# The experts' down product in three one-pass products of high and low parts, in place of one plain product

## The reference

```python
def expert_block(args):
    xb, e = args          # 128 token rows, 1024 wide; weights 1024x512, 1024x512, 512x1024
    return (jax.nn.silu(xb @ w_gate[e]) * (xb @ w_up[e])) @ w_down[e]
```

## Time and profile before

| | |
|---|---|
| runs, us | 1544.82, 1678.39, 1680.1 |
| median of the runs | 1678.39 us |
| profiled execution, span from first to last instruction | 1678.9 us |
| TensorE busy | 1494.5 us (89%) |
| VectorE busy | 923.6 us (55%) |
| ScalarE busy | 586.6 us (35%) |
| DMA | 353.18 MB, mean 210 GB/s |
| mean granted TensorE clock | 0.857 |

### The profile page before, as it was taken

How to read it: one execution, slowest core, us unless ns; L and a number is a source line. 1 busy time by engine, 2 the same in 40 slices (tenths; PEclk the granted TensorE clock), 3 DMA queues, 4 the chain that set the end, 5 groups by cost and what they waited for, 6 DMA issues and landing times.

```text
span 1678.9 us, 15037 instructions
## 1 busy us (share of the span) xinstructions
PE 1494.5 (89%) x5233; PEld 977.5 (58%) x5233; DVE 923.6 (55%) x1344; ACT 586.6 (35%) x790; POOL 91.4 (5%) x133
## 2 busy tenths in 40 slices
PE   2899999399999998499989999999956999999892
PEld 2445455266667764288866666666535677766540
DVE  6588824667777771566642222222356777777304
ACT  1265002355555550322122222221234555555201
POOL 4000000100000000200000000000001000000001
PEclk9999999599999999699995555555977999999996
DMA  8946680369999987456370000000033999999644
GB/s 279 365 161 211 200 314 38 124 236 363 374 360 368 385 317 287 163 176 238 103 284 27 0 1 0 0 1 1 25 138 126 365 371 370 369 364 347 238 163 163
DMA packets 79747, 353.18 MB, mean 210 GB/s; under 512 B 12824, under 2 KB 13008, under 8 KB 70736
## 3 DMA queue, kind: packets, MB, share of 16 engines
q1 hardware_dynamic: 64704, 326.65, 52.6%
q0 software_dynamic: 8352, 20.46, 3.4%
q10 hardware_dynamic: 6640, 5.42, 1.0%
HBM read 334.15 MB, written 28.31 MB: 216 GB/s over the span
## 4 chain that ended last, share of the span: by engine, by line
PE 87%; DVE 6%; ACT 2%; DMA 2%; issue 2%; ACTq 1%; POOL 0%; DVEq 0%; POOLq 0%; SPq 0%
PE ps L1533 21%; PE ps L1544 14%; PE ps L1446 9%; PE ps L1632 8%; PE ps L1662 7%; PE ps L1474 7%; PE ps L1673 6%; PE ps L1687 4%; PE ps L1524 3%; PE ps L1519 2%; PE ps L1420 2%; PE ps L1538 1%; PE ps L1487 1%; PE ps L1456 1%; ACTq L636 1%
## 5 line engine op out<-in xcount | busy, mean ns | idle before, releaser
L1544 PE MATMUL ps<-slab_ring,scratch 128*128 128x512 f32 x560 | 246.5, 593 | 3.4 <-ACT scratch L783 2.1
L1533 PE MATMUL ps<-slab_ring_r,gate_rows_r 128*128 128x512 f32 x512 | 202.2, 395 | 0.0
L1544 PEld LDWEIGHTS ps<-slab_ring,scratch 128*128 128x128 f32 x560 | 105.8, 190 | 124.2 <-issue 117.3
L1229 DVE TENSOR_TENSOR slab_ring_r<-slab_ring,h_t_r 128x2048 fp32r<-128x2048 f32 x64 | 143.8, 2288 | 22.7 <-ACT h_t_r L735 22.7
L1364 DVE CUSTOM_DVE_ANT_0 mod_ring<-ps,log_count 128x512 f32<-128x512 f32 x64 | 44.2, 691 | 197.0 <-PE ps L1662 197.0
L1446 PE MATMUL ps<-h_t,slab_ring 128*128 128x512 f32 x320 | 146.1, 617 | 0.0
L1662 PE MATMUL ps<-h_t,scratch 64*128 64x512 f32 x128 | 127.4, 1106 | 0.9 <-DVE h_t L1355 0.9
L1632 PE MATMUL ps<-slab_ring_r 128*128 128x512 f32 x384 | 123.6, 404 | 1.7 <-DVE h_t_r L902 1.7
L817 ACT ACTIVATE mod_ring<-mod_ring,neg_max 128x512 f32<-128x512 f32 x64 | 46.2, 722 | 217.9 <-DVE neg_max L1365 217.9
L1533 PE MATMUL ps<-h_t_r,gate_rows_r 128*128 128x512 f32 x256 | 106.3, 415 | 14.7 <-DVE scratch_r L1223 14.7
L735 ACT ACTIVATE h_t_r<-slab_ring 128x2048 fp32r<-128x2048 f32 x64 | 118.4, 1901 | 0.2 <-issue 0.2
(11 more groups left out here) (286 smaller groups left out, 2200.2 us busy)
## 6 DMA issues: line engine op xcount, KB each, us to landing
slab_ring<-in_expert_w_gate_dram SPq DMA_DIRECT2D x35, 2048.0 KB, 10.3
slab_ring<-in_expert_w_up_dram SPq DMA_DIRECT2D x35, 2048.0 KB, 10.2
slab_ring<-in_expert_w_down_dram SPq DMA_DIRECT2D x35, 2048.0 KB, 10.4
mod_ring<-in_mod_w_dram SPq DMA_DIRECT2D x64, 512.0 KB, 4.7
y_rows<-scratch SPq DMA_DIRECT2D x35, 512.0 KB, 10.8
slab_ring<-in_mod_w_dram SPq DMA_DIRECT2D x32, 512.0 KB, 4.7
slab_ring<-in_w_qkv_dram SPq DMA_DIRECT2D x6, 2048.0 KB, 11.9
slab_ring<-in_w_in_ab_dram SPq DMA_DIRECT2D x5, 2048.0 KB, 19.3
```

Of the source, the lines that this page charges most:

```text
L1229: tt_(rest, w, top.bitcast(F32), ALU.subtract).then_inc(low_ready[c], 1)
L1533: ins = pe.matmul(ps[:, bank, :], x, w, start=(kt == 0 and i == 0), stop=(kt == KT - 1 and i == 2))
L1544: ins = pe.matmul(ps[:, 5 + h, :], hidT[:, f, :], w[:, 2 * f + h, :], start=(f == 0), stop=(f == FT - 1))
```

## The change

Down is split as gate and up are. Its slab gets a high part from ScalarE (in the buffer of the two, `XN_r` or `modr_r`, that up does not use in that layer) and a low part in place from VectorE, in two chunks each; both stand last in the queue of step e. The copy of the turned hidden out of PSUM now writes a high part (`hidT_high`), and VectorE computes a low part from PSUM minus this (`low_hid`), between the two chunks of low of up. TensorE does three one-pass products in place of each plain one, and waits for `hidt_low` and for the two low chunks of down in place of the slab. The overflow blocks keep the plain product. Some semaphores of the overflow code (`over`, `seen`) are merged into `turn_seen`.

```diff
--- before.py
+++ after.py
@@ -140,7 +140,9 @@
     ybuf = [R[:, 9:11, :].rearrange("p a n -> p (a n)"), R[:, 11:13, :].rearrange("p a n -> p (a n)")]
     xs_low = [R_r[:, i:i + 2, :].rearrange("p a (b n) -> p (a b) n", n=P) for i in (4, 13)]
     xs_high = [[G_r[:, g, :].rearrange("p (a n) -> p a n", n=P) for g in gs] for gs in ((0, 2), (1, 2))]
-    w_high = [[HT_r, (XN_r[:, :, :].rearrange("p t (h n) -> p (t h) n", h=2), modr_r)[l]] for l in range(LAYERS)]
+    XN_halves = XN_r[:, :, :].rearrange("p t (h n) -> p (t h) n", h=2)
+    w_high = [[HT_r, (XN_halves, modr_r)[l], (modr_r, XN_halves)[l]] for l in range(LAYERS)]
+    hidT_high, hidT_low = (R_r[:, i, :].rearrange("p (f n) -> p f n", n=P) for i in (8, 15))
     rt = R[:, 13:16, :].rearrange("p a n -> p (a n)")
     place_hot = R_r[:, 9:11, :].rearrange("p a (t n) -> p (a t) n", n=P)
     block_tok = R_r[:, 11, 0:2 * TT * WIDE].rearrange("p (a b) -> p a b", b=WIDE)
@@ -245,7 +247,8 @@
     xn_stored, place_ready, slots_summed, slots_ready = sem("xn_stored"), sem("place_ready"), sem("slots_summed"), sem("slots_ready")
     xs_filled = [sem("xs_filled0"), sem("xs_filled1")]
     xs_turned, xst_act, xst_dve = sem("xs_turned"), sem("xst_act"), sem("xst_dve")
-    high_ready, low_ready = [sem("gate_high"), sem("up_high")], [sem("gate_low"), sem("up_low")]
+    high_ready, low_ready = [sem("gate_high"), sem("up_high"), sem("down_high")], [sem("gate_low"), sem("up_low"), sem("down_low")]
+    hidt_low = sem("hidt_low")
     xs_high_ready, xst_turned, xst_split = sem("xs_high_ready"), sem("xst_turned"), sem("xst_split")
     gate_done, up_done, silu_done = sem("gate_done"), sem("up_done"), sem("silu_done")
     hid_ready, hid_turned, hidt_ready = sem("hid_ready"), sem("hid_turned"), sem("hidt_ready")
@@ -254,7 +257,7 @@
     turn_seen = sem("turn_seen")
     y_zeroed = sem("y_zeroed")
     comb_filled = [sem(f"comb_filled{t}") for t in range(TT)]
-    over = [{n: sem(f"over{l}_{n}") for n in ("wg", "wu", "wd", "xs", "turned", "xst", "gu", "silu", "hid", "hidt_in", "hidt", "down", "yb", "stored", "step", "over", "seen", "gate")}
+    over = [{n: sem(f"over{l}_{n}") for n in ("wg", "wu", "wd", "xs", "turned", "xst", "gu", "silu", "hid", "hidt_in", "hidt", "down", "yb", "stored", "step", "gate")}
             for l in range(LAYERS)]
     qkv_high, qkv_low, qkv_chunk = sem("qkv_high"), sem("qkv_low"), sem("qkv_chunk")
     ht_full, ht_high_act, ht_high_dve = sem("ht_full"), sem("ht_high_act"), sem("ht_high_dve")
@@ -459,7 +462,7 @@
                     sp.wait_ge(o["yb"], k + 1)
                     sp.dma_start(y_dram[bass.ds((k + NE) * P, P), :], ybuf[0]).then_inc(o["stored"], 16)
                     sp.wait_ge(o["stored"], (k + 2) * 16)
-                    sp.sem_inc(o["over"], 1)
+                    sp.sem_inc(turn_seen, 1)
             for par in range(2):
                 sp.wait_ge(yb_stored[par], 16 * (NE // 2) * (l + 1))
 
@@ -575,7 +578,7 @@
             def gather_over(k):
                 gp.tensor_copy(idx[0][:, :], slot_tok[:, bass.ds(k + NE, 1)]).then_inc(o["step"], 1)
                 gp.wait_ge(o["step"], k + 1)
-                gp.sem_inc(o["seen"], 1)
+                gp.sem_inc(turn_seen, 1)
                 gp.indirect_dma_start(out=xs[0], out_offset=None, in_=xn_dram,
                                       in_offset=bass.IndirectOffsetOnAxis(ap=idx[0][:, 0:1], axis=0),
                                       bounds_check=S - 1, oob_is_err=False).then_inc(o["xs"], 16)
@@ -730,7 +733,7 @@
 
                 wait_slab(act, ("exp", l, c, par), turn)
                 if not first:
-                    act.wait_ge((gate_done, up_done)[c], e + e0)
+                    act.wait_ge((gate_done, up_done, down_done)[c], e + e0)
                 w, top, _ = split_of(l, c, par, chunk)
                 act.activation(top, w, ACT.Copy).then_inc(high_ready[c], 1)
 
@@ -739,7 +742,7 @@
                 act.wait_ge(hid_turned, e + (e0 + 1))
                 if not first:
                     act.wait_ge(down_done, e + e0)
-                act.activation(hidT, ps[:, 4, :].rearrange("p (f n) -> p f n", n=P), ACT.Copy).then_inc(hidt_ready, 1)
+                act.activation(hidT_high, ps[:, 4, :].rearrange("p (f n) -> p f n", n=P), ACT.Copy).then_inc(hidt_ready, 1)
 
             def step(e, par, turn, first=0, last=False):
 
@@ -755,6 +758,8 @@
                     for chunk in range(2):
                         high(0, e + 1, 1 - par, turn + par, chunk)
                     xst(e + 1, 1 - par, first == 1)
+                for chunk in range(2):
+                    high(2, e, par, turn, chunk, first == 1)
 
             for chunk in range(2):
                 high(0, 0, 0, 0, chunk, True)
@@ -1240,9 +1245,16 @@
                     v.wait_ge(yb_stored[par], stored * 16 + (NE // 2) * l * 16)
                 scale_y(ybuf[par], yb_ready)
 
+            def low_hid(e):
+
+                v.wait_ge(hidt_ready, e + (e0 + 1))
+                tt_(hidT_low, ps[:, 4, :].rearrange("p (f n) -> p f n", n=P), hidT_high.bitcast(F32), ALU.subtract).then_inc(hidt_low, 1)
+
             def step(e, par, stored=None, first=False, last=False):
-                for chunk in range(2):
-                    low(1, e, par, chunk)
+                low(1, e, par, 0)
+                if not first:
+                    low_hid(e - 1)
+                low(1, e, par, 1)
                 if not last:
                     for chunk in range(2):
                         low(0, e + 1, 1 - par, chunk)
@@ -1253,6 +1265,8 @@
                 v.wait_ge(silu_done, e + (e0 + 1))
                 v.wait_ge(up_done, e + (e0 + 1))
                 tt_(hid, ps[:, 3, :], sg, ALU.mult).then_inc(hid_ready, 1)
+                for chunk in range(2):
+                    low(2, e, par, chunk)
 
             for chunk in range(2):
                 low(0, 0, 0, chunk)
@@ -1266,6 +1280,7 @@
                 step(2 * i + 1, 1, i)
             step(NE - 2, 0, NE // 2 - 2)
             step(NE - 1, 1, NE // 2 - 1, last=True)
+            low_hid(NE - 1)
             take_y(NE - 1, 1, NE // 2 - 1)
 
             o = over[l]
@@ -1550,10 +1565,16 @@
 
             def down_product(e, par, turn, first=False):
                 pe.wait_ge(hidt_ready, e + (e0 + 1))
+                pe.wait_ge(hidt_low, e + (e0 + 1))
                 if not first:
                     pe.wait_ge(yb_ready, e + e0)
-                wait_slab(pe, ("exp", l, 2, par), turn)
-                down(slab(("exp", l, 2, par)), down_done)
+                pe.wait_ge(low_ready[2], 2 * e + (2 * e0 + 2))
+                for h in range(2):
+                    for f in range(FT):
+                        w_top, w_rest = w_high[l][2][:, 2 * f + h, :], w_low(l, 2, par)[:, 2 * f + h, :]
+                        for i, (x, w) in enumerate(((hidT_high, w_top), (hidT_high, w_rest), (hidT_low, w_top))):
+                            ins = pe.matmul(ps[:, 5 + h, :], x[:, f, :], w, start=(f == 0 and i == 0), stop=(f == FT - 1 and i == 2))
+                ins.then_inc(down_done, 1)
 
             def step(e, par, turn, first=0, last=False):
```

## The result

The changed kernel took 1594.55, 1589.39, 1586.4 and 1727.48 us (median 1591.97); the kernel before, run beside it, 1544.82, 1678.39, 1680.1 and 1543.22 (median 1611.61). Both kernels come at two levels, 135 us apart before and 137 after, and three of the four new runs lie on the lower one. Level against level the change makes the kernel slower: ratio 1.0299, interval 1.0234 to 1.0363. That is 1590.1 against 1544.0 in the mean of the lower runs (+46), and 1727.5 against 1679.2 in the upper (+48).

A forecast was written before the change was run, and what follows sets the result against it. The prediction took TensorE to bound the kernel now and VectorE's queue to hold down back after the change: 1678.9 + 35 (28 steps) - 2 (first experts) + 8 (layer ends) = 1720 us; own range 1704 to 1745, 8 in 10 within 1580 to 1750.

The forecast's parts named there:

- The base: Whole kernel: the sum starts from the profile's span, 1678.9 us, 0.5 us from the median, not from the listed 1544.82.
- rival 2: Attention: TensorE runs at 2.4 GHz there, 134 us less, giving 1586 us; chance 0.19.
- The forecast's own range: Whole kernel: 1704 to 1745 us, from periods between 20.15 and 20.8 us and the clock at the ends.
- Down at 5.5 us: Down product on TensorE: 24 one-pass products take 5.5 us against 6.87, 1.4 us less per expert.
- Low of the hidden through at 8.2: VectorE's queue: the turned hidden's low part ends 8.2 us after up's end; down starts at 8.3, now 5.71.
- Period 20.4: Expert step: 8.3 + 12.05 = 20.4 us against 19.16, +1.25 per expert, 28 times: 35 us.
- VectorE's floor: Expert step: VectorE's work becomes 14.29 + 4.49 + 0.6 = 19.4 us, more than the present period of 19.16.
- Rival 4: Expert steps: VectorE's sum alone decides, 19.4 us per expert, giving 1692 us; chance 0.10.
- Rival 1: Expert stages: the clock falls in the new 2.5 us pauses, 1.64 us each, 46 in all, giving 1766; chance 0.14.
- The end of a layer: Last expert: +2.4 us for uncovered work and +1.6 for the clock, +4.0 per layer, +8 together.
- Rival 3: Expert steps: TensorE keeps the bound, each step 1.4 us shorter, 39 us in all, giving 1640; chance 0.05.
- First expert: Expert 1 of each layer: down starts 0.4 us later and is 1.4 shorter, -1 us, -2 for both layers.

The follow-up runs named there:

- e5: The kernel before with four unread plain products in TensorE's pauses at the attention's entry; median 1545.63 us, ratio 1.0011 to the lower runs of before.
- e1: The changed kernel with VectorE's low of the hidden ahead of both low chunks of up; 1535.58 us on the lower level, 1666.4 to 1669.4 on the upper.
- e2: The kernel before with TensorE's part alone: down as 24 one-pass products, nothing added on VectorE or ScalarE; 1499.79 to 1502.01 and 1632.13 us, ratio 0.9736.
- e8: e7 with two tiles of turned inputs moved to ScalarE, two through another PSUM bank, and the last expert's low of down earlier; median 1518.49 us, ratio 0.9839.
- e6: The changed kernel with four unread plain products in TensorE's pauses at the attention's entry; median 1591.87 us, ratio 1.0324 to the lower runs of before.
- e7: e1 with four unread plain products in TensorE's pauses at the attention's entry; median 1536.98 us, ratio 0.9962 to the lower runs of before.
- e3: The changed kernel with one plain down product in place of the three one-pass ones, all new copies, subtractions and waits kept; 1789.79 to 1793.03 us, ratio 1.066.
- e9: e6 with VectorE's low of the hidden one place later, behind both low chunks of up; 1694.11 to 1697.52 us, 104.5 more than e6.
- e10: e6 with two unread plain products ahead of each down, four ahead of a layer's last; 1580.32 to 1583.13 us, ratio 1.0243, 9.3 below e6.

## Why the prediction was wrong in its number and right in its mechanism

- **The base, the step that failed.** "So I set the sum against 1678.9": one run in three was at 1544.82, and I took the profile's level for the level to come. Over all runs of the kernel before in this study 16 of 38 were on the upper level, of the kernel after 1 of 4. The two are modes of the same program, and the forecast for a median had to split its chance between them by their share; 0.19 for rival 2 was too little, even by the one in three that I had. As a price rival 2 was right: 1720 - 134 = 1586, and 1590 measured. Its reason was not: it had the change move the moment at which the attention begins, but the kernel before alone has both levels, and e5 took the upper one away without moving anything ahead of the attention. The range, 1580 to 1750, was drawn down to rival 2 and holds the time; that is no merit of the sum. The forecast's own range, 1704 to 1745, is also some 5 us wider at each end than its terms: a period of 20.15, which nothing in the text leads to, gives 1709 without any loss of clock, and 20.8 with the full loss gives 1739.
- **What the change adds on its own base: right.** +41 us forecast, +46 to +48 measured. Down at 5.5 us: 5.70 behind a pause, 5.45 without one. Low of the hidden through at 8.2: at 8.0. Pause of 2.5: 2.2 and 2.4. Period 20.4 (+1.25): 20.3 (+1.16) where the clock holds. The two kinds of step, 20.2 and 20.4 us from down to down, differ by the hand-over alone: from the end of VectorE's subtraction to the start of down are 0.10 us in one and 0.34 to 0.38 in the other, where the sum had 0.1. The longer one belongs to one of the two experts of a pass through the loop, and is not there in the last two steps, which stand outside it; what makes it is open.
- **VectorE's floor: wrong.** "That makes 19.4 us per expert: already more than the 19.16 of now, so TensorE's 1.4 us can't be had." e1 has the same work in 18.6, and the changed kernel has VectorE busy for 18.62 us of a step where the prediction looked for 19.3. Durations were added where starts had to be (some 0.5 of the 0.8 us), and the 0.25 of the shorter conversion could not be seen from the kernel before. It did not spoil the forecast, since the order and not the sum bound the step; but it hid that the change loses by one place in a queue. Rival 4 rested on that floor and fell with it.
- **Rival 1, the clock in the pauses: partly.** Four of the 28 steady down products and both at the ends were slower by it. The end of a layer, from the last hidden product to the end of down, was forecast at +4.0 and was +4.7 in layer 0 (9.24 to 13.91 us) and +5.1 in layer 1 (9.24 to 14.33). The wait and the shorter product make +2.3 of it, as in the sum (+2.4); the mis-sized term is the clock, 2.4 and 2.8 (8.12 and 8.53 against 5.70) where the sum had 1.6.
- **Rival 3, TensorE keeps the bound: false here, for the reason given**, the queue. e2 shows what it would have brought, 40 us, and e8 how much of it is to be had.
- **First expert:** by the timeline its down starts 0.4 later in layer 0, as forecast (25.17 us behind the first gate product, against 24.81), and no later in layer 1. It is 1.2 shorter in the chain of waits (1.4 forecast).

## What to carry to other kernels

When a change adds work to an engine that others wait for, write down its queue from the event that releases it, by starts and not by durations, and put the operation that the critical engine waits for first: one place in the queue was worth 55 us here (e6 to e7), and one place the other way 104. If the times listed for a kernel lie on two levels, forecast on both and give each its share; a few unread products in the pauses in which the clock falls made the level constant here, and then differences of half a per cent could be seen. Moving elementwise work to an idle engine is a gain only if the two engines can run side by side: look at that first.

## What I had not expected of the hardware

- Pauses of the same length do not have the same effect on TensorE's clock. Behind 2.2 to 2.4 us it fell from 2.4 to 1.2 GHz in 4 of 28 cases in the kernel after, in 3 of 28 in e6, and in 20 of 28 in e3, where plain products stand in place of the 24 one-pass ones; behind 4.4 to 4.6 us (e9) in 28 of 28; behind 0.5 to 0.7 (e10) in none. In e3 it is the fourth, seventh, eleventh and fourteenth down product of the layer that kept the clock, in both layers alike. What tells the four from the 24 is open.
- The attention fell to 1.2 GHz and stayed there in 16 of 38 runs of the kernel before (told by the time and by the mean granted clock of the run, 0.86 against 0.94; the profile shows it for one), and in none of the 36 runs of the six kernels with the four products.
- A subtraction of 128x2048 on VectorE beside one on POOL takes 6.12 us in place of 2.28. It goes the other way too: POOL's copy of an index column, 128x1, takes 0.18 us in the kernels before and after, and 1.46 in e1, where it starts at 515.26 and ends at 516.72, next to the end of a VectorE subtraction at 516.67 (the two from 512.18 for 4.49).
